# Values spread from SBUF to SBUF on ACT's queue, a merge that starts with the attention branch, output weights split inside the merge, and an opening without a ring

## The reference, cut to what matters

```python
hx = modulate(rmsnorm(x, norm1_g), sh1, sc1)        # sh1, sc1: silu(c) @ w_mod + b_mod
zx = hx @ w_in + b_in                               # Hyena inputs, q, k, v, two gates
hy = hyena_mixer(zx[:, :1536], ...)                 # short convolution, two long convolutions
na = neighbourhood_attention(q, k, v, kc, vc, rpb)  # 8 heads, windows 8 x 16, plus context
mix = (sigmoid(g_hy) * (hy @ w_branch_hy) + sigmoid(g_na) * (na @ w_branch_na)) @ w_out
x = x + g1 * mix
h2 = modulate(rmsnorm(x, norm2_g), sh2, sc2)
x = x + g2 * expert_choice_ffn(h2)                  # 16 experts, 128 tokens each, SwiGLU
out = rmsnorm(x, final_g)
```

## Time and profile before

| | |
|---|---|
| median of 3 runs | 2705.07 us (2698.1 to 2707.09) |
| the profiled execution's own time | 2703.3 us |
| its span | 2700.7 us |
| PE busy | 2545.6 us, 94% of the span |
| DVE busy | 2121.3 us, 79% |
| ACT busy | 1469.9 us, 54% |
| POOL busy | 149.3 us, 6% |
| granted clock of PE, mean | 0.973 |

### The profile page before, as it was taken

One profiled execution on the slowest core, in us unless ns is written; L12 is line 12 of the kernel. 1 busy time (PEld: TensorE's weight loads), 2 busy tenths in 40 slices (PEclk: granted clock), 3 DMA queues, 4 the chain that ended last, 5 costly groups with the idle time before them and its releaser, 6 DMA issues.

```text
span 2700.7 us, 32209 instructions
## 1 busy us (share of the span) xinstructions
PE 2545.6 (94%) x12577; PEld 2121.3 (79%) x12577; DVE 2121.3 (79%) x1976; ACT 1469.9 (54%) x1249; POOL 149.3 (6%) x159
## 2 busy tenths in 40 slices
PE   6999979999999899389999999999999999999997
PEld 2777869878878778368888888888888888888885
DVE  5674247667879555688888888889888888888887
ACT  4522136531121222177777777777777777777774
POOL 0011000011111000000000000000000000000000
PEclk9999989999999999689999999999999999999998
DMA  7498774464566733399999999999999999999994
GB/s 272 161 314 306 248 228 111 135 200 140 162 200 197 236 104 131 155 339 362 386 390 373 374 392 381 363 383 394 370 373 392 380 366 383 389 375 367 392 382 171
DMA packets 198628, 794.93 MB, mean 294 GB/s; under 512 B 17935, under 2 KB 65399, under 8 KB 128528
## 3 DMA queue, kind: packets, MB, share of 16 engines
q1 hardware_dynamic: 168196, 704.75, 69.4%
q0 software_dynamic: 30128, 88.11, 10.6%
q10 hardware_dynamic: 158, 0.07, 0.0%
HBM read 723.38 MB, written 69.48 MB: 294 GB/s over the span
## 4 chain that ended last, share of the span: by engine, by line
PE 53%; ACT 2%; issue 2%; DVE 1%; DVEq 0%; ACTq 0%
PE moe_ps_gate L2210 18%; PE moe_ps_up L2210 16%; PE moe_ps_y L2200 16%; PE moe_ps_h L2181 2%; ACT moe_w_hi L2251 1%; PE moe_ps_x L2173 1%; DVE raw L2373 0%; ACT moe_xt_hi L2244 0%; DVE moe_w_lo L2303 0%; DVE moe_h L2324 0%; ACT moe_sl L2264 0%; DVE raw L2360 0%; PE moe_ps_gate L2234 0%; PE moe_ps_gate L2236 0%; PE moe_ps_up L2234 0%
## 5 line engine op out<-in xcount | busy, mean ns | idle before, releaser
L2303 DVE TENSOR_TENSOR moe_w_lo<-raw,moe_w_hi 128x2048 fp32r<-128x2048 f32 x528 | 1207.6, 2290 | 159.8 <-ACT moe_w_hi L2251 159.6
L2251 ACT ACTIVATE moe_w_hi<-raw 128x2048 fp32r<-128x2048 f32 x528 | 1011.0, 1919 | 379.2 <-PE moe_ps_gate L2210 128.4
L2210 PE MATMUL moe_ps_up<-moe_w_hi,moe_xt_hi 128*128 128x512 f32 (+1 forms) x768 | 292.4, 381 | 0.0
L2210 PE MATMUL moe_ps_gate<-moe_w_hi,moe_xt_hi 128*128 128x512 f32 (+1 forms) x768 | 289.1, 376 | 1.4 <-DVE moe_xt_lo L2294 1.4
L2210 PE MATMUL moe_ps_gate<-moe_w_hi,moe_xt_lo 128*128 128x512 f32 (+1 forms) x768 | 286.5, 373 | 0.0
L2210 PE MATMUL moe_ps_up<-moe_w_hi,moe_xt_lo 128*128 128x512 f32 (+1 forms) x768 | 286.4, 373 | 0.0
L2210 PE MATMUL moe_ps_gate<-moe_w_lo,moe_xt_hi 128*128 128x512 f32 (+1 forms) x768 | 286.1, 373 | 0.0
L2210 PE MATMUL moe_ps_up<-moe_w_lo,moe_xt_hi 128*128 128x512 f32 (+1 forms) x768 | 285.9, 372 | 0.0
L2200 PE MATMUL moe_ps_y<-moe_w_hi,moe_ht_hi 128*128 128x512 f32 x704 | 218.5, 392 | 0.0
L2200 PE MATMUL moe_ps_y<-moe_w_hi,moe_ht_lo 128*128 128x512 f32 x704 | 217.0, 389 | 0.0
L2200 PE MATMUL moe_ps_y<-moe_w_lo,moe_ht_hi 128*128 128x512 f32 x704 | 217.0, 389 | 0.0
(11 more groups left out here) (278 smaller groups left out, 3707.1 us busy)
## 6 DMA issues: line engine op xcount, KB each, us to landing
raw<-in_w_moe SPq DMA_DIRECT2D x528, 1024.0 KB, 7.2
hyena_g_parts<-gw_d POOLq DMA_DIRECT2D x64, 512.0 KB, 4.7
proj_w_mod<-in_w_mod SPq DMA_DIRECT2D x32, 512.0 KB, 7.3
gw_d<-proj_g_parts POOLq DMA_DIRECT2D x16, 1024.0 KB, 7.4
w_in<-in_w_in SPq DMA_DIRECT2D x12, 1024.0 KB, 7.6
attn_table<-in_na_table SPq DMA_DIRECT2D x16, 576.0 KB, 5.6
norm_w_mod<-in_w_mod SPq DMA_DIRECT2D x16, 512.0 KB, 7.1
proj_g_raw<-in_w_in SPq DMA_DIRECT2D x16, 512.0 KB, 9.5
```

The source lines that it names most:

```text
L2210: mm = pe.matmul(ps, hp[:, e % 2, k, :], wp[:, r, :], start=(k == 0 and x == 0), stop=(k == KD - 1 and x == 2))
L2251: act.activation(w_hi[:, g % PARTS], raw[:, g % RAW], ACT.Copy).then_inc(hi_ready, 1)
L2303: dve.tensor_tensor(w_lo[:, g % PARTS], raw[:, g % RAW], w_hi[:, g % PARTS].bitcast(F32), ALU.subtract).then_inc(lo_ready, 1)
```

## The change

- **Opening:** the ring is gone. All four chunks have places of their own, SP issues all pieces without waiting for PE, PE waits for whole chunks (for pieces in the last one), and the bias row of the values is loaded just ahead of them.
- **Values:** `v_d` is gone. ACT issues eight transfers of 64 KB for each latent tile, from `v_stage` in SBUF to `v_band` in SBUF, for tiles 0 to 6 at the end of its list. SP issues those of tile 7 at the head of the attention block. DVE fills a slot of `v_stage` again when the spread of the tile before last has landed.
- **Merge:** in the last pass of the convolution SP loads the first branch weights and the attention's output, ACT and DVE split the first weights and the first quarter of that output, and ACT the other three quarters after it. The merge's first chunk starts with the attention branch. Its loops are written out.
- **Output weights:** the first four steps of the split of `w_out` go between the chunks of the merge, and so does the first tokens' split.
- **Fillers:** 18 transposes of the identity (`FILL`) at the end of the convolution and of the merge, and 36 (`WARM`) at the start of the experts. Their results are not used.
- **Experts:** the second half of the first tokens turns through another PSUM tile, the first unit waits for the first half alone, DVE splits two units before the halves, and the first `multiply` comes earlier.

The core of the diff:

```diff
-def load_values(sp, a, keep, kg):
-    for b in range(4):
-        for r in range(4):
-            first = (4 * kg + r) * GRID_W + BAND_AT[b]
-            sp.dma_start(keep["v_band"][BAND * r:BAND * (r + 1), v_block(kg, b), 0:HEADS * HD],
-                         a["v_d"][first:first + BAND]).then_inc(keep["v_in"][kg // 3], 16)
...
+    kg, v_stage = t // 2, keep["v_stage"]
+    for r in range(2):
+        row = 2 * (t % 2) + r
+        for b in range(4):
+            first = r * GRID_W + BAND_AT[b]
+            eng.dma_start(keep["v_band"][row * BAND:(row + 1) * BAND, v_block(kg, b), 0:HEADS * HD],
+                          v_stage[first:first + BAND, t % 2]).then_inc(keep["v_in"][t % 2], 16)
+def spread(t):
+    return 128 * (t // 2 + 1)
...
-                    if n:
-                        sp.wait_ge(piece_used, PIECES * (n - 1) + q + 1)
-                    sp.dma_start(w_early[:, q], mod_src[n, q]).then_inc(w_mod_in[q], 16)
+                    sp.dma_start(w_early[:, n, q], mod_src[n, q]
+                                 ).then_inc(last_piece_in[q] if n == NC - 1 else w_mod_in[n], 16)
...
-                for kg in range(3):
-                    for x in range(2):
-                        sp.wait_ge(stored[x], 16 * (SEG_V[0] + kg + 1))
-                    load_values(sp, a, keep, kg)
...
-                for t in range(TT):
-                    pool.wait_ge(evacuated, V_AT + 2 + t + 1)
-                    pool.dma_start(a["v_d"][t * P:(t + 1) * P], v_stage[:, t % 2]).then_inc(stored[t % 2], 16)
...
+                        pe.wait_ge(w_mod_in[n], CHUNK_IN)
                     for q in range(PIECES):
...
+                for t in range(TT - 1):
+                    act.wait_ge(evacuated, V_AT + 2 + t + 1)
+                    spread_values(act, keep, t)
...
+                dve.wait_ge(bv_in, AFTER_PIECE + 16)
...
-                            dve.wait_ge(stored[t % 2], 16 * (SEG_V[0] + t // 2))
+                            dve.wait_ge(keep["v_in"][t % 2], spread(t - 2))
...
-                for x in range(2):
-                    sp.wait_ge(stored[x], 16 * (SEG_V[0] + 4))
-                load_values(sp, a, keep, 3)
+                spread_values(sp, keep, TT - 1)
...
-                        pe.wait_ge(v_in[g], 16 * 48 if g == 0 else 16 * 16)
+                        for t in ((TT - 4, TT - 3) if g == 0 else (TT - 2, TT - 1)):
+                            pe.wait_ge(v_in[t % 2], spread(t))
...
+                        if p == PASSES - 1 and r == 1:
+                            sp.wait_ge(tap_used, PH * PASSES)
+                            sp.wait_ge(a_done, a_at["seg", p, PH - 1] + 1)
+                            for b, w in enumerate(branch_sources(a)):
+                                sp.dma_start(coming["b_raw"][:, 0, b], w[0]).then_inc(branch_in[0], 16)
+                            for k in range(NA_SLOTS):
+                                load_na(k)
...
+                load_na(NA_SLOTS)
...
+                for _ in range(FILL):
+                    pe.transpose(ps_a[:, 0, 0:P], ident[:], ident[:])
...
+                def high_na(k):
+                    act.wait_ge(na_in, 16 * max(NA_SLOTS, k + 1))
+                    act.activation(coming["hi"][1][:, k], coming["na_raw"][:, k % NA_SLOTS], ACT.Copy
+                                   ).then_inc(na_hi_ready, 1)
...
+                    if p == PASSES - 1:
+                        act.wait_ge(branch_in[0], 32)
+                        act.activation(coming["b_hi"][:, 0], coming["b_raw"][:, 0], ACT.Copy).then_inc(bh_ready, 1)
+                        act.wait_ge(out_done, NB * p)
+                        high_na(0)
...
+                for k in range(1, 4):
+                    high_na(k)
...
                     dve.sem_inc(y_ready, 1)
...
+                    if p == PASSES - 1:
+                        dve.wait_ge(bh_ready, 1)
+                        dve.tensor_tensor(coming["b_lo"][:, 0], coming["b_raw"][:, 0], coming["b_hi"][:, 0].bitcast(F32),
+                                          ALU.subtract).then_inc(bl_ready, 1)
+                        low_na(dve, coming, 0)
...
-                            pe.wait_ge(in_lo_ready, 4 * b + k + 1)
+                            pe.wait_ge(in_lo_ready, k + 1 if b else 4 + k + 1)
...
-                branch(0, 0, 0, first=True)
-                branch(0, 1, 0)
+                branch(0, 0, 1, first=True)
+                branch(0, 1, 1)
                 for th in range(2):
-                    branch(0, th, 1, first=not th).then_inc(branched, 1)
+                    branch(0, th, 0, first=not th).then_inc(branched, 1)
...
+                pe.wait_ge(merged, 2 * KD + 1)
+                for _ in range(FILL):
+                    pe.transpose(ps[:, 0, 0, 0:P], keep["ident"][:], keep["ident"][:])
...
+                for k in range(4):
+                    act.activation(in_hi[0][:, k, :], y_t[:, k, :], ACT.Copy).then_inc(in_hi_ready, 1)
+                for d in range(1, KD):
+                    split(d % 2, d // 2, d)
+                    if d == OUT_FROM:
+                        act.wait_ge(in_lo_ready, 8)
+                    if d >= OUT_FROM and d - OUT_FROM < 4:
+                        k = d - OUT_FROM
+                        act.wait_ge(keep["wo_in"][0], 32)
+                        act.activation(keep["out_w_hi"][0][:, k, :], keep["wo_raw"][:, k, :], ACT.Copy
+                                       ).then_inc(keep["wo_hi"], 1)
...
+                for k in range(1, 4):
+                    low_na(dve, at, k)
+                for k in range(4):
+                    dve.wait_ge(in_hi_ready, 4 + k + 1)
+                    dve.tensor_tensor(in_lo[0][:, k, :], y_t[:, k, :], in_hi[0][:, k, :].bitcast(F32),
+                                      ALU.subtract).then_inc(in_lo_ready, 1)
+                for d in range(KD):
+                    if d + 1 < KD:
+                        split(d + 1, (d + 1) % 2)
+                    gated(d, 0)
+                    if d == KD - 1:
+                        dve.wait_ge(merged, 4 + 2 * d + 1)
+                        split_tokens(dve, dt, keep, m_t, 0, 0)
+                    gated(d, 1)
+                    if d >= OUT_FROM and d - OUT_FROM < 4:
+                        low_out(dve, keep, d - OUT_FROM)
+OUT_FROM = 3
+FILL = 18
...
+def split_tokens(dve, dt, keep, m_t, t, s):
+    src = m_t[:, :, bass.ds(t * P, P)] if not isinstance(t, int) else m_t[:, :, t * P:(t + 1) * P]
+    hi, lo = keep["out_m_hi"][s], keep["out_m_lo"][s]
+    dt.then_wait(dve.tensor_scalar(hi[:], src, 1.0, None, ALU.mult))
+    dve.tensor_tensor(lo[:], src, hi[:].bitcast(F32), ALU.subtract).then_inc(keep["m_split"], 1)
...
+def low_out(dve, keep, k):
+    dve.wait_ge(keep["wo_hi"], k + 1)
+    dve.tensor_tensor(keep["out_w_lo"][k // 4][:, k % 4, :], keep["wo_raw"][:, k, :],
+                      keep["out_w_hi"][k // 4][:, k % 4, :].bitcast(F32), ALU.subtract).then_inc(keep["wo_lo"], 1)
...
-                for k in range(KD):
-                    act.wait_ge(wo_in[k // 4], 32)
-                    act.activation(w_hi[:, k, :], w_raw[:, k, :], ACT.Copy).then_inc(wo_hi, 1)
+                act.wait_ge(wo_in[1], 32)
+                for k in range(4, KD):
+                    act.activation(w_hi[1][:, k - 4, :], w_raw[:, k, :], ACT.Copy).then_inc(wo_hi, 1)
...
-                split(0, 0)
-                for k in range(KD):
-                    dve.wait_ge(wo_hi, k + 1)
-                    dve.tensor_tensor(w_lo[:, k, :], w_raw[:, k, :], w_hi[:, k, :].bitcast(F32), ALU.subtract
-                                      ).then_inc(wo_lo, 1)
+                for k in range(4, KD):
+                    low_out(dve, keep, k)
...
+            return ps_h if (e, half) == (0, 1) else ps_x
...
-                if LAST_OF["up", c] + PARTS - soon == v:
+                if LAST_OF["up", c] + (3 if first and c == 0 else PARTS - soon) == v:
...
-                    if half or e:
+                    if e:
                         pe.wait_ge(x_parts, 2 * e + half)
...
+                        mm = pe.transpose(x_turned(e, half)[:, k * P:(k + 1) * P], xe[:, at:at + P], ident[:])
...
+                    else:
+                        pe.wait_ge(x_parts, 2)
...
+                for n in range(WARM):
+                    pe.transpose(ps_x[:, n % 4 * P:(n % 4 + 1) * P], ident[:], ident[:])
...
-                    pe.wait_ge(x_parts, 2 * e + 2)
+                    if e:
+                        pe.wait_ge(x_parts, 2 * e + 2)
...
+                        if e == 0 and u < 2:
+                            pe.wait_ge(x_parts, u + 1)
...
-                for g in range(AHEAD):
+                split(0)
+                split(1)
+                for half in range(2):
+                    low_x(0, half)
+                for g in range(2, AHEAD):
                     split(g)
...
-                low_x(0, 0)
-                low_x(0, 1)
```

188 lines of the change are left out of this document (101 added, 87 removed).

## The result

The changed kernel takes 2687.49 us (median of 6 runs, 2684.45 to 2691.22), the kernel before 2701.47 on the same chips. The ratio is 0.9949, with a 95% interval of 0.9934 to 0.9964: faster by 0.5%, or 14 us. The forecast was 2670, 1.2% faster. The range of 2662 to 2688 just holds the time, but the gain is 14 us where 33 were forecast. The profiled execution has a span of 2689.1 us, 11.6 less than before. It took 2691.22 us, the longest of the six, so its stretches are a little long.

A forecast was written before the change was run, and what follows sets the result against it. PE, busy 94% of the span, was taken as the bound, with gains only where it waits or runs at half clock. Gains of 1.6 + 12.9 + 0.8 + 7.0 + 4.1 + 6.5 = 32.9 took 2703.3 to 2670 us; range 2662 to 2688.

The forecast's parts named there:

- the end of the projection: Values block before the attention: without SP's 64 reloads it ends at 360.1 instead of 373.0, gain 12.9 us.
- the spread of a tile: End of the projection: write 0.7, issues 3.6 and landing 5.9 make 10.2 us, fitting a slot's 11.
- Rival C: End of the projection: slow spreads or late input stores end the block at about 365, gain 8, time 2675; chance 0.12.
- Rival D: End of the projection: SP still ends near 373 because of its stores, only 20.0 gained, 2683 us; chance 0.05.
- Rival E: Projection's values: each spread lands in 22.2 us, DVE waits for slots, 13.6 us slower, 2717 us; chance 0.06.
- Start of the attention: Attention's first products: PE no longer starts cold after its long wait, gain 0.8 us, between 0 and 1.5.
- Merge: Start of the merge: earlier splits and a warm clock remove PE's 8.97 us gap and cold start, gain 7.0 us.
- Output projection: Its start: earlier weight and token splits and a warm first product, gain 4.1 us, bounds 2 and 5.7.
- T + 15.2: Output projection: forecast time of the second tile's split on DVE, T being the start of the merge's last product.
- Experts: Start of the experts: halves alone give 4.2 us and warm products 2.3, gain 6.5, bounds 2.3 and 7.
- Opening: Modulation at the start: without the ring DVE adds row 3 directly behind its split, gain 1.6 us, bounds 0 and 3.
- Rival B: Filler transposes don't raise or hold PE's clock; 2674.5 us, or 2678 if other starts are cold too; chance 0.25.

The follow-up runs named there:

- Experiment 1: Changed kernel with SP's stores of the normalised input moved to about 80 us, away from the spreads; 2676.49 us.
- Experiment 2: Changed kernel with the input's stores at 80 us and the spreads of tiles 1, 3 and 5 issued by SP instead of ACT; 2675.41 us.
- experiment 8: Changed kernel with the old opening put back: the ring's waits for loads, PE waiting for single pieces; 2686.89 us.
- experiment 6: Changed kernel without its filler transposes, FILL and WARM both at 0; 2688.04 us.
- experiment 5: Changed kernel with 26 transposes of the identity on PE in the opening's wait for the last modulation row; 2685.17 us.

## Why the prediction was wrong

**The step that failed** is the end of the projection, forecast at −12.9 and measured at −0.4. The term that broke in it is the spread of a tile: 3.6 us for its eight issues and 5.9 for its landing, 9.5 in all. The third tile's spread was issued in 11.3 us, and DVE could write its slot again 17.3 us after the first issue (334.98 to 352.31). The landing was near its term, 6.6 us at the median; the issues took three times theirs. Three things in the working led there.
- *The cover.* "They start before 336.78 and have some 20 us" was said of the input's stores, but only to ask whether they end in time. They run from 319 to 358 us, the stretch in which most of the tiles are spread, and the sum never priced the issues beside them. An issue took up to 2.1 us, 1.75 at the mean around 350 us, where ACT's 0.31 and SP's 0.45 to 0.6 were taken. Experiment 1 shows it: without the stores the distance falls from 14.2 to 4.3.
- *The price of an issue.* Free of the stores it is 0.64 us, so eight take 5.1, above the 2.5 to 4.8 of the working and only 0.4 under a tile's 5.5. One queue can then not make up for a slot that is once 3 us late. Experiment 2 removes that as well, and the distance is 1.6; the forecast had 1.7.
- *The size.* "A spread of 256 KB" is what a tile holds. Its eight transfers of 64 KB carry 512 KB, because neighbouring bands overlap. No run tells what this alone cost.

Rival C had this mechanism at 0.12, but priced it at 5 us. Rival D had the time of this place, at 0.05, by another cause (SP). Rival E had the waits for slots in line, from the second tile on, but by a landing of 22.2 us and not by the issues. The sum was too hopeful because the earlier trace rows gave POOL's store at 5.9 us in the same stretch, and I took it as proof that a transfer is quick beside the stores. It is one transfer with one issue; a spread is eight that ACT issues one by one, and from the third tile on each issue was slowed. Why the issues of the first two tiles were not, beside the same stores, no run shows.

**The other steps.** *Start of the attention*, −0.8: nothing, since the block still ended late; experiment 2 shows the 0.8 once the wait is gone. *Merge*, −7.0: right to 0.1 us (98.2 to 91.2), although `FILL` has only 0.5 of it. The loads "counted as nothing" cost some 0.9 in the last pass: PE waited 2.6 us there for the gates' parts, and not at all before, while a wait of 1.7 us for DVE in front of the last output products is gone. *Output projection*, −4.1: 1.0 in this execution and 3 in most. The order of events was as written, with DVE's split as what is late; it came at T + 16.5 instead of T + 15.2, the router's weights having taken 8.4 us to land instead of 7.1, and PE fell to half clock in the wait, which the sum left out. *Experts*, −6.5: measured −5.1. The first product came 4.6 us sooner behind the indices, `WARM` gave 2.6, and 1.95 went into a wait that the sum did not have, `moe_ht_lo` behind five weight splits on DVE. *Opening*, −1.6, measured +1.1: DVE's row came where it was forecast (41.34), and the gap of PE in front of it cost the clock. I had asked what the earlier row gives and not what PE does until then. The row's place in the kernel before was itself one execution's: 43.4 there, 41.8 in experiment 8 with the same waits, where the last value product came at 357.1, no later than with the changed opening.

**Rival B** is refuted. The clock rose from 0.50 to 1.00 during 36 transposes of the identity (experiment 6). The Trainium skill, "TensorE: Matmul & The Clock Gate", section "Part 4: PE-mode transpose", says that transposes do not bring the full clock; this trace does not agree.

So of the 21 us between forecast and measured span, 13.3 lie in the values with the attention's start, 2.7 in the opening, 0.9 in the stretch with the last pass, 3.1 in the output projection and 1.4 in the experts. About 2 us in the opening and 2 in the output projection are this execution's own: three of the seven others with the changed opening did not lose them there, and seven of the eight others with the same output projection did not lose them there.

## What to carry to other kernels

Before a transfer is moved to another queue, list what the transfer engines carry in that stretch, and price both its issue and its landing beside it: here an unrelated store of 8 MB, which could go 240 us earlier at no cost, hid the whole gain. Then compare the issuing queue with the pace of the work: a queue that is only a few per cent faster can't make up for one late slot. Ask of every place where work comes earlier what the engine does until then, for a gap of 2 to 3 us on PE can cost 2 us of half clock behind it. Effects of 1 to 2 us are read from the distance between two marks in a trace, and from several traces, for the same code gave 26.3 to 29.2 us in one such distance here; medians of whole runs don't show them one by one, only in sum.

## What the runs showed of the hardware

- A DMA issue on ACT's queue isn't of fixed length: 0.64 us each in a free stretch, 1.75 us each around 350 us, while 8 MB of another queue's stores were moving at some 400 GB/s. Beside the same stores the first sixteen still took 0.5 to 0.75 us. The transfers behind it in the list go out as much later.
- Two queues issued 56 transfers of 64 KB in time where one could not, with the same 2.0 to 2.1 us to landing once the other transfers were done. So it was the issuing that was short, not the path.
- Transposes alone raised PE's clock from 1.2 to 2.4 GHz (0.50 to 1.00 in the windows of experiment 6), and 26 of them in a gap kept it there (experiment 5).
- Executions of one opening differ by up to 3 us in when the last row is added (40.2 to 43.2). Behind it the clock stayed low for 3 to 10 us, and 10 us of it cost 2 us.
